# Reading a matmul's 512 moving columns in interleaved runs of 16, 64 and 4 columns

## The reference

```
# first block
up = causal_dwconv(h @ w_up, conv_w, conv_b)        # w_up: 2048 x 11264
a, b = up[..., :FFN_DIM], up[..., FFN_DIM:]         # FFN_DIM = 5632
x = x + (silu(a) * b) @ w_down                      # w_down: 5632 x 2048
...
# second block
gt, up = jnp.split(rms_norm_2(x, g_ffn) @ w_gate_up, 2, axis=-1)   # 2048 x 11264
return x + (jax.nn.silu(gt) * up) @ w_down                         # 5632 x 2048
```

## Time and profile before

| what | value |
|---|---|
| the two executions | 2978.95 us, 2976.33 us |
| span of the profiled execution | 2978.0 us |
| TensorE (PE) busy | 2946.2 us, 99% |
| PE's weight loads busy | 2630.0 us, 88% |
| VectorE (DVE) busy | 2051.0 us, 69% |
| ScalarE (ACT) busy | 1311.7 us, 44% |
| chain that ended last, PE's share | 96% |
| bytes read | 526.94 MB, 178 GB/s over the span |

### The profile page before, as it was taken

One profiled execution on the slowest core, in us unless ns is written; L12 is line 12 of the kernel. 1 busy time (PEld: TensorE's weight loads), 2 busy tenths in 40 slices (PEclk: granted clock), 3 DMA queues, 4 the chain that ended last, 5 costly groups with the idle time before them and its releaser, 6 DMA issues.

```text
span 2978.0 us, 47097 instructions
## 1 busy us (share of the span) xinstructions
PE 2946.2 (99%) x18616; PEld 2630.0 (88%) x18616; DVE 2051.0 (69%) x2624; ACT 1311.7 (44%) x1418; POOL 70.0 (2%) x72
## 2 busy tenths in 40 slices
PE   8999999999999999999999999999999999999999
PEld 8898898999988888888888888876998888888888
DVE  6675787977788888885557776636666666666444
ACT  5354423444444444444444354425445444444333
POOL 0000000000001000000000000000000000000000
PEclk9999999999999999999999999999999999999999
DMA  6553334555555555555555544531555555555555
GB/s 230 184 183 134 114 120 149 168 173 198 186 196 193 189 196 194 190 182 190 193 195 198 195 172 168 186 122 43 184 198 186 195 197 188 193 197 177 194 193 184
DMA packets 87359, 530.39 MB, mean 178 GB/s; under 512 B 9952, under 2 KB 10336, under 8 KB 41184
## 3 DMA queue, kind: packets, MB, share of 16 engines
q1 hardware_dynamic: 87264, 529.07, 50.7%
HBM read 526.94 MB, written 2.10 MB: 178 GB/s over the span
## 4 chain that ended last, share of the span: by engine, by line
PE 96%; DVE 2%; ACT 1%; DMA 0%; issue 0%; SPq 0%; DVEq 0%; ACTq 0%
PE bank L576 74%; PE late L576 22%; DVE arena L1687 1%; DVE w_low L1687 0%; DVE half_low L1687 0%; DVE arena L1684 0%; ACT w_high L1203 0%; PE late L1144 0%; DVE arena L1989 0%; DMA ring<-in_w_gates 0%; DMA xT<-in_xT 0%; DVE acts_both L1687 0%; DVE arena L2045 0%; DVE arena L2016 0%; DVE xrs L1734 0%
## 5 line engine op out<-in xcount | busy, mean ns | idle before, releaser
L1687 DVE TENSOR_TENSOR w_low<-ring,w_high 128x2048 fp32r<-128x2048 f32 (+1 forms) x480 | 1014.3, 2113 | 384.1 <-ACT w_high L1203 380.2
L1203 ACT ACTIVATE w_high<-ring 128x2048 fp32r<-128x2048 f32 (+1 forms) x480 | 849.5, 1771 | 636.0 <-DMA ring<-in_w_down 223.0
L576 PE MATMUL bank<-up_early,w_high 128*128 128x512 f32 x1408 | 487.8, 389 | 0.0
L576 PE MATMUL bank<-up_late,w_high 128*128 128x512 f32 x1408 | 487.3, 389 | 0.0
L576 PE MATMUL late<-acts_both,w_high 128*128 128x512 f32 x1408 | 479.0, 389 | 0.3 <-DVE w_low L1687 0.3
L576 PE MATMUL bank<-up_early,w_low 128*128 128x256 f32 x1408 | 388.6, 276 | 0.0
L576 PE MATMUL late<-acts_both,w_low 128*128 128x256 f32 x1408 | 388.6, 276 | 0.0
L576 PE MATMUL bank<-up_late,w_low 128*128 128x256 f32 x1408 | 388.6, 276 | 0.0
L576 PEld LDWEIGHTS bank<-up_early,w_high 128*128 128x128 f32 x1408 | 264.5, 188 | 55.2
L576 PEld LDWEIGHTS late<-acts_both,w_high 128*128 128x128 f32 x1408 | 264.3, 188 | 55.1 <-DVE w_low L1687 0.6
L576 PEld LDWEIGHTS bank<-up_late,w_high 128*128 128x128 f32 x1408 | 264.0, 188 | 54.7
(11 more groups left out here) (311 smaller groups left out, 4946.2 us busy)
## 6 DMA issues: line engine op xcount, KB each, us to landing
ring<-in_w_up SPq DMA_DIRECT2D x176, 1024.0 KB, 4.7
ring<-in_w_down SPq DMA_DIRECT2D x128, 704.0 KB, 4.0
ring<-in_w_in SPq DMA_DIRECT2D x66, 1024.0 KB, 4.7
ring<-in_w_mix SPq DMA_DIRECT2D x62, 1024.0 KB, 4.8
ring<-in_w_gates SPq DMA_DIRECT2D x96, 512.0 KB, 3.7
ring<-in_w_branch SPq DMA_DIRECT2D x16, 1024.0 KB, 4.7
ring<-in_w_out SPq DMA_DIRECT2D x16, 1024.0 KB, 4.8
ring<-in_w_o SPq DMA_DIRECT2D x16, 1024.0 KB, 4.8
```

The costliest lines, as they stand in the source:

```text
L576: return nc.tensor.matmul(o, lhsT, rhs, start=first, stop=last)
L1203: A(w_high[:, s, 0:cols], ring[:, s, 0:cols], ACT.Copy).then_inc(rounded[s], 1)
L1687: return V.tensor_tensor(o, a, b, op)
```

## The change

A constant `RUNS = (16, 64, 4, 0)` is added, and a helper that reorders the view of an operand [128, 2, 256]: with a run of v columns the matmul takes v columns of the first part, then v of the second, then the next v of the first, and so on. The same view is laid over the output in PSUM, so that every value goes where it went before. The values, the number of matmuls, their 512 columns, the weight loads and the semaphores are those of before.

The first up projection gets runs of 16 columns, the first down projection 64, the second up projection 4. The second down projection has 0, which leaves it as it was; so are the output and input projections, which also use `project_pairs`. The 256-column matmuls are not touched. As built, an instruction `bank<-up_early,w_high 128x512` becomes `128x16x2x16` in the first up projection, and `late<-acts_both,w_high` becomes `128x4x2x64` in the first down projection; their places in PE's stream, and the instructions of all other engines, stay in the same order. (In `acts_both` the low part is first in memory, in `ups` the high part.)

```diff
+RUNS = (16, 64, 4, 0)
...
-            def project_pairs(pairs, waits=None):
+            def in_turn(x, run):
+
+                return x.rearrange("p a (u v) -> p u a v", v=run) if run else x
+
+            def project_pairs(pairs, waits=None, run=0):
...
-                        mm(bank[s][:], w_high[:, s, c], pairs[k], k == 0, False)
+                        mm(in_turn(bank[s][:], run), w_high[:, s, c], in_turn(pairs[k], run), k == 0, False)
                         last = mm(bank[s][:, 0], w_low[:, s, c], pairs[k][:, 0], False, k == KT - 1)
...
-            def down(m):
+            def down(m, run):
...
-                                mm(bank[4 + b][:], w_high[:, s, c], acts_both[:, :, n], n == 0, False)
+                                mm(in_turn(bank[4 + b][:], run), w_high[:, s, c],
+                                   in_turn(acts_both[:, :, n], run), n == 0, False)
                                 last = mm(bank[4 + b][:, 1], w_low[:, s, c], acts_high[:, n], False, n == FF_TILES - 1)
...
-            raw_unit(lambda waits: project_pairs(ups, waits))
+            raw_unit(lambda waits: project_pairs(ups, waits, RUNS[0]))
             for j in range(3):
-                unit_split(project_pairs(ups))
-            rounds_split(21, project_pairs(ups))
-            down(0)
+                unit_split(project_pairs(ups, run=RUNS[0]))
+            rounds_split(21, project_pairs(ups, run=RUNS[0]))
+            down(0, RUNS[1])
...
-            raw_unit(lambda waits: project_pairs(ups, waits))
+            raw_unit(lambda waits: project_pairs(ups, waits, RUNS[2]))
             for j in range(3):
-                unit_split(project_pairs(ups))
-            rounds_split(21, project_pairs(ups))
-            down(1)
+                unit_split(project_pairs(ups, run=RUNS[2]))
+            rounds_split(21, project_pairs(ups, run=RUNS[2]))
+            down(1, RUNS[3])
```

## The result

The changed kernel takes 3050.57 us (3049.52 to 3051.63) against 2977.64 us before: a ratio of 1.0249, with an interval of 1.0230 to 1.0269. It is slower by 2.5%. The time lies in the forecast range, but the forecast of no change was wrong, and rival A, with the chance 0.20, comes nearest. The span of the profiled execution is 3047.7 us, 69.7 more than before.

The account below looks back on a forecast made before the run. PE's matmul pace was taken to bound the up and down projections. 3520 reordered pairs times 0 added gave 0, so the forecast stayed at the median, 2977.6 us, with a range of 2931 to 3072.

Parts of the forecast that it names:

- the forecast of no change: Three reordered stages: the 3520 pairs keep 0.3400 us each, so the time stays 2977.6 us; chance 0.50.
- rival A: Mainly second up: short runs slow PE or the accumulating memory; +95 us, 3072, or +285 us, 3263; chance 0.20.
- What bounds the kernel: In the up and down projections, 1418.1 us in four pieces, PE alone sets the end.
- What does one cost? ... So I take 0.: In the reordered stages, each of 227,392 changes of place between the two operand parts costs 0.
- one cycle at each change: Upper bound in the reordered stages: 0.417 ns for each of 227,392 changes, +95 us, 73 of it in second up.
- Its test, an excess in the ratio of 127 to 31: Second up's excess over first up's should be near 127 to 31 if each change of place costs the same.
- Rival B: All three reordered stages or stretches: pairs go at 0.3500, +35 us, 3013, or 0.3594, +68 us, 3046; chance 0.11.
- In every case the second down must stay at 239.4 us; if it moves, my reading is wrong.: The second down's 704 untouched pairs served as the control, expected to stay at 239.4 us.
- That the 256-column matmul keeps its pace: In the reordered pairs, the sum counted only what the new order adds to the 512-column matmul's 0.2267 us.
- Rivals C and D: C: the 13.3 ns vanish in changed matmuls, -47 us, 2931, chance 0.17; D: building straightens the view, 2977.6, chance 0.02.
- The 13.3 ns lost in 512 straight columns: A 512-column matmul takes 226.7 ns against 213.3 at one column per cycle; the difference was unnamed.

Follow-up runs that it names:

- experiment 4: The changed kernel with the runs on the output in PSUM only, the moving operand read straight; 2976.46 us.
- experiment 1: The changed kernel with only the first up projection reordered, in runs of 16, the other stages straight; 3004.40 us.
- experiment 2: The changed kernel with only the second up projection reordered, in runs of 4, the other stages straight; 3029.06 us.
- experiment 11: The kernel before, with PE waiting at each output tile of both down projections until the previous tile has left its bank; 3023.01 us.
- experiment 10: The changed kernel with the operand's second part filled with values as large as those of the first; 3046.43 us.
- experiment 5: The changed kernel with the second matmul of a pair loading 32 columns of low weights instead of 128, in all but the last of each bank; 3055.50 us.
- experiment 9: The changed kernel with only the up projections reordered, in runs of 16 and 4, all even blocks first, then all odd; 3018.11 us.

## Why the prediction was wrong

*What bounds the kernel* was right: every nanosecond of pace became a nanosecond of the end. 72.0 us in four PE pieces explain the 69.7 of the span, with 3 us back elsewhere, and PE doesn't idle in them. (The 2978.0 us of the profile before were put down to the execution of 2978.95; in every other run the span is 1.7 to 2.1 us below its time, so it was more likely a third execution. Nothing hangs on it.)

*"What does one cost? ... So I take 0."* This is the step that failed. The rows compared one jump in 512 columns with none, and from that said nothing about 31 or 127. I wrote down the objection, and chose the row over it. In its place the runs showed +20 ns a pair at 16 columns, +26.7 at 4 and 0 at 64, so 27.8 + 37.1 + 0 us. The doubt had been given a price, one cycle at each change or +95 us; the measured sum is inside it. But this was luck in part. The price was laid out in proportion to the changes, 18 us for the first up and 75 for the second (the working's 73 is a slip: 1408 x 127 x 0.417 ns is 74.5), and the two came out at 28 and 37. So one cycle at each change was no upper bound: a change cost 0.65 ns in runs of 16 and 0.9 in runs of 32, and the sum stayed inside only because runs of 4 paid 0.21. A matmul that changes place 31 times loses three quarters of what one with 127 changes does.

*Rival A* had the sign and a time near the measured one, but its place was half wrong. It put the loss in the second up above all, and named the accumulating memory beside PE as a cause; experiment 4 excludes the memory. Its test, an excess in the ratio of 127 to 31, failed with 37.1 to 27.8.

*Rival B*, the other pace, was counted as an alternative, and came in addition: +7.0 us in the second down. It depends on which stream ran ahead and on the last idle gap (experiments 1, 2, 11). The rows that showed it, 0.3500 beside 0.3406 for the same pairs, were in the prediction; what I didn't draw from them is that an untouched stage can pick it up.

*"In every case the second down must stay at 239.4 us; if it moves, my reading is wrong."* It moved, and this sentence did its work. The control was no control, since it follows the second up without a gap; experiment 1 gave a clean one.

*That the 256-column matmul keeps its pace* was assumed in the sum, which spoke of what the order adds to 0.2267 alone. It goes from 276 to 282 ns through the engine in the up projections though its own pattern is straight. By the starts in the trace, its distance to the next matmul in the first up went from 113 to 120 or 121 ns, and that of the 512-column matmul from 227 to 239 or 240: a third of the loss falls on the matmul that wasn't changed. So the price must be read by pairs.

*Rivals C and D*: of the changed matmuls none got faster in any run, and the new view is walked, or nothing would have changed. The 13.3 ns lost in 512 straight columns aren't explained. They aren't due to the values (experiment 10). Whether the weight load beside them has a part is open: with the shorter one a straight stream went at 0.3468, between its two paces (experiment 5).

What stays open: which part of the reading path loses the time, why its prices are 13, 20, 21 and 27 ns for 32, 16, 8 and 4 columns, and what decides between 0.3400 and 0.3500 after a gap. What the weight load adds outside runs of 16 is open too. That reading is the place is shown; a mechanism behind it is not.

## What to carry to other kernels

Where PE bounds a stage of pairs like these, give the moving operand runs of 64 32-bit values or more, and never under 4; in the output in PSUM, runs of 4 were as good as straight columns. A row that shows one jump for free doesn't price 31 of them: when nothing in the trace has the new pattern, the sum's middle should move towards the bound. And compare untouched stages by piece of the chain before using one as a control: in a back-to-back stream the pace is partly inherited.

## What the runs showed of the hardware that was not expected

- A back-to-back stream of the same matmuls has two exact paces, 0.3400 and 0.3500 us a pair here, at a granted clock of 1.00 in both. It takes one of them after idle time (about 15.27 or 15.68 us for 44 pairs), keeps it over hundreds of pairs and over a foreign matmul put in between, and a stage can take over 0.3500 from a slower one that runs into it without a gap (experiments 1 and 2), though behind experiment 9's even and odd runs of 4 the second down had 0.3400. Over one down projection this is 7 us, 0.24% of the kernel.
- The paces come out the same to 0.01 us in stretches of 500 us in different kernels (501.13 five times, 510.41 four times), so they are no noise.
- Going from runs of 4 to runs of 2 values costs 80 ns a pair at once (0.3667 to 0.4467), three times what all shorter steps from 64 to 4 cost together.
